# Attention with 64-row scores and normalised probabilities, norms by logarithm, and alternating output panels

## What is computed

```python
def first_block(x, ...):
    u = rmsnorm(h, norm_mix_g[layer])
    p = jnp.einsum('bsd,de->bse', u, w_in[layer]) + b_in[layer]
    aq, ak, av, hq, hf, hi, hg, gate_a, gate_b = split_columns(p)
    y_attn = sliding_window_sink_attention(aq, ak, av, attn_sinks[layer])
    y_hgrn = hgrn2_branch(hq, hf, hi, hg, lb_all[layer], hgrn_norm_g[layer])
    ya = jnp.einsum('bse,ed->bsd', y_attn, w_branch_attn[layer])
    yb = jnp.einsum('bse,ed->bsd', y_hgrn, w_branch_hgrn[layer])
    merged = jax.nn.sigmoid(gate_a) * ya + jax.nn.sigmoid(gate_b) * yb
    h = h + jnp.einsum('bsd,de->bse', merged, w_out[layer])
...
    # attention: a softmax over the keys and one sink
    probs = jax.nn.softmax(jnp.concatenate([scores, sink], axis=-1), axis=-1)[..., :-1]
    out = jnp.einsum('bhgqk,bnkhd->bnqhgd', probs.astype(v.dtype), vw)
...
    # end of the HGRN2 branch; the SSD mixer ends in a norm of the same form
    o = o * lax.rsqrt(jnp.mean(o * o, axis=-1, keepdims=True) + EPS)
    o = o.reshape(B, S, HGRN_WIDTH) * norm_g.astype(jnp.float32)
    o = o * jax.nn.sigmoid(hg.astype(jnp.float32))
```

## Time and profile before

| | us |
|---|---|
| median of 3 runs | 902.66 |
| lowest and highest | 901.04 and 906.4 |
| the profiled execution | 902.78 |
| its span on the core | 900.9 |
| TensorE busy | 838.6 |
| VectorE busy | 597.4 |
| ScalarE busy | 480.6 |

### The profile page before, as it was taken

How to read it: one execution, slowest core, us unless ns; L and a number is a source line. 1 busy time by engine, 2 the same in 40 slices (tenths; PEclk the granted TensorE clock), 3 DMA queues, 4 the chain that set the end, 5 groups by cost and what they waited for, 6 DMA issues and landing times. The chain is left out here.

```text
span 900.9 us, 14307 instructions
## 1 busy us (share of the span) xinstructions
PE 838.6 (93%) x5976; PEld 784.8 (87%) x5976; DVE 597.4 (66%) x754; ACT 480.6 (53%) x709; POOL 25.8 (3%) x43
## 2 busy tenths in 40 slices
PE   7999999969896989999999989998969899999996
PEld 6999989969895979999998879887947899999885
DVE  5554666477748748777779987674444588887653
ACT  6747768446633436344433456724443477666542
POOL 3400001000100000000000000000000000000000
PEclk9999999988998999999999998989979999999999
DMA  9644544426531555888778965533410386655621
GB/s 316 235 162 143 165 135 145 165 96 231 159 124 47 188 187 194 282 273 280 257 261 287 343 254 188 177 104 101 133 48 1 111 269 203 189 165 187 209 96 47
DMA packets 105952, 161.15 MB, mean 179 GB/s; under 512 B 4496, under 2 KB 51872, under 8 KB 105888
## 3 DMA queue, kind: packets, MB, share of 16 engines
q1 hardware_dynamic: 105888, 160.24, 53.6%
HBM read 159.16 MB, written 1.06 MB: 178 GB/s over the span
## 5 line engine op out<-in xcount | busy, mean ns | idle before, releaser
L1469 PE MATMUL ps<-p1H,wH 128*128 128x256 f32 x1256 | 366.0, 291 | 21.1 <-DVE wL L965 9.0
L965 DVE TENSOR_TENSOR wL<-raw,wH 128x2048 fp32r<-128x2048 f32 (+2 forms) x129 | 281.8, 2187 | 154.8 <-ACT wH L652 153.8
L1469 PE MATMUL ps<-p1L,wH 128*128 128x256 f32 x1256 | 360.8, 287 | 0.0
L1469 PE MATMUL ps<-p1H,wL 128*128 128x256 f32 x1256 | 360.6, 287 | 0.0
L652 ACT ACTIVATE wH<-raw 128x2048 fp32r<-128x2048 f32 (+1 forms) x124 | 231.3, 1869 | 152.5 <-PE ps L1469 75.1
L1469 PEld LDWEIGHTS ps<-p1H,wH 128*128 128x128 f32 x1256 | 246.5, 196 | 24.7 <-DVE wL L965 9.4
L1469 PEld LDWEIGHTS ps<-p1L,wH 128*128 128x128 f32 x1256 | 246.6, 196 | 0.4 <-issue 0.2
L1469 PEld LDWEIGHTS ps<-p1H,wL 128*128 128x128 f32 x1256 | 246.2, 196 | 0.0
L1472 PE MATMUL ps<-wH,zH 128*128 128x512 f32 x176 | 68.7, 390 | 0.0
L1472 PE MATMUL ps<-wL,zH 128*128 128x512 f32 x176 | 68.5, 389 | 0.0
L1472 PE MATMUL ps<-wH,zL 128*128 128x512 f32 x176 | 68.5, 389 | 0.0
(11 more groups left out here) (257 smaller groups left out, 1011.0 us busy)
## 6 DMA issues: line engine op xcount, KB each, us to landing
raw<-in_w_in SPq DMA_DIRECT2D x38, 1024.0 KB, 5.2
raw<-in_w_ada SPq DMA_DIRECT2D x24, 1024.0 KB, 5.3
raw<-in_w_up SPq DMA_DIRECT2D x44, 512.0 KB, 4.9
raw<-in_w_ffn_gate SPq DMA_DIRECT2D x22, 512.0 KB, 4.4
raw<-in_w_ffn_up SPq DMA_DIRECT2D x22, 512.0 KB, 5.5
raw<-in_w_ffn_down SPq DMA_DIRECT2D x10, 1024.0 KB, 5.6
raw<-in_w_down SPq DMA_DIRECT2D x10, 1024.0 KB, 5.1
raw<-in_w_out SPq DMA_DIRECT2D x8, 1024.0 KB, 5.1
```

What stands on the lines that cost most here:

```text
L965: return v.tensor_tensor(o, a, b, op)
L1469: last = mm(ps[:, t[1], 0:T], wt[:, slot, k, t[2]:t[2] + P], at_[:, k0 + k, :], start=st, stop=en)
```

## The change

*Attention.* The keys are no longer padded: the product of a head contracts over its 64 rows. The two heads of a pair lie in different halves of the rows and of the PSUM banks (`slot`), and the masks of both are written first. For keys that lie in the wrong half a swapped copy `aKS` is made. The value product has the values stationary, 64 columns for each head of a pair, and comes out transposed, so the item "yT" and its instructions are gone and "pv" does the split. The probabilities are normalised on VectorE in place, in the item "pt", ahead of TensorE's transposes, which now wait for `on.pn`. *Norms of the mixers.* HGRN2 and SSD take Ln and Exp(-0.5 x) on ScalarE for square root and reciprocal; the HGRN2 gain comes first (hD) and the product with the norm in an item of its own (hE); the split is done in halves. *Panels.* bh0 and bh1, and oo0 and oo1, alternate panel by panel, bh1 in PSUM banks 4 to 7. *Places.* Scores 7 stand ahead of pv 6; scores 8 are split in two (`scores_mm` for TensorE, ahead of the SSD sums); dt comes half a group earlier; a norm's gate sums and spreads come earlier with one copy for 256 columns instead of two for 128; the squares of norm 3 stand ahead of the evacuation of oo1; a low part of the first weights moves from GpSimd to VectorE; the ada item of f0 is gone and one stands behind part 4 of down1; the sums of ada move from f2, f4, f6, f8 to f3, f5, f7, f9. The line numbers after are higher by 3 to 14 (L965 becomes L971, L1415 becomes L1418, L1469 becomes L1480).

```diff
 def X(u):
     return [("pv", u - 1)] * (u > 0) + [("scores", u)] * (u < NU1)
 def Y(u):
-    return [("pt", u)] * (u < NU1) + [("yT", u - 1)] * (u > 0)
+    return [("pt", u)]
...
-    gemm("hq1", [("hD", 0)])
+    gemm("hq1", [("hD", 0)], [("hE", 0)])
...
-    gemm("ba1", [("hC", 1)], [("hsplit", 0), ("hD", 1), ("hsplit", 1)])
-    gemm("bh0")
-    gemm("bh1", [("merge", 0)], [("merge", 1)])
+    gemm("ba1", [("hC", 1)], [("hsplit", 0), ("hD", 1)])
+    gemm("bh0", [("hE", 1), ("hsplit", 1)], only=0)
+    gemm("bh1", only=0)
+    gemm("bh0", [], [("merge", 0)], only=1)
+    gemm("bh1", [], [("merge", 1)], only=1)
...
-    gemm("v2", [("pt", 6)], [("pv", 6), ("scores", 7)])
-    gemm("z", [("pt", 7), ("yT", 6)], [("pv", 7), ("yz",), ("scores", 8), ("ysum",), ("snorm",)])
-    gemm("oo0", [("pt", 8), ("yT", 7), ("pv", 8), ("yT", 8)])
-    gemm("oo1", [("squares", 3)], [("gate", 1), ("norm", 3)])
+    gemm("v2", [("pt", 6)], [("scores", 7), ("pv", 6)])
+    gemm("z", [("pt", 7)], [("pv", 7), ("yz",), ("scores_mm", 8), ("ysum",), ("snorm",), ("scores", 8)])
+    gemm("oo0", [("pt", 8)], only=0)
+    gemm("oo1", [("pv", 8)], only=0)
+    gemm("oo0", only=1)
+    gemm("oo1", [], [("norm", 3)], only=1)
...
-WITH_ADA += [(f"f{_i}", 0) for _i in range(NF)]
-WITH_ADA += [("down0", _i) for _i in range(1, 6)] + [("down1", _i) for _i in range(4)]
+WITH_ADA += [(f"f{_i}", 0) for _i in range(1, NF)]
+WITH_ADA += [("down0", _i) for _i in range(1, 6)] + [("down1", _i) for _i in range(5)]
...
-                elif k == "pv":
+                elif k == "pt":
                     u = e[1]
                     dve.wait_ge(on.probs, u + 1)
...
                     step(v.reciprocal(RD[:, u % 2, 0:nh], SU[:, u % 2, 0:nh]))
-                    dve.wait_ge(on.pv_psum, u + 1)
-                    if u:
-                        dve.wait_ge(on.yT_psum, u)
-                    tt(YT[:, 0:nh * DH].rearrange("p (h d) -> p h d", h=nh),
-                           ps[:, 6, 0:nh * DH].rearrange("p (h d) -> p h d", h=nh),
-                           RD[:, u % 2, 0:nh].unsqueeze(2).broadcast_to([P, nh, DH]), ALU.mult).then_inc(on.pv_done, 1)
+                    p = PR.rearrange("p (h b) n -> p h (b n)", h=nh)
+                    tt(p, p, RD[:, u % 2, 0:nh].unsqueeze(2).broadcast_to([P, nh, nk * P]), ALU.mult).then_inc(on.pn, 1)
...
                 elif k == "hD":
                     s = e[1]
+                    dve.wait_ge(on.o_sq, 2 * s + 2)
+                    for h in range(4):
+                        stt(T1[:, h], T1[:, h], pc("hgrn_norm_g", 4 * s + h), hG[:, h],
+                            ALU.mult, ALU.mult).then_inc(on.o_gain, 1)
+                elif k == "hE":
+                    s = e[1]
+                    dve.wait_ge(on.o_gain, 4 * s + 4)
                     for i in range(2):
-                        dve.wait_ge(on.o_rt, 2 * s + i + 1)
-                        step(v.reciprocal(T2[:, 2 * i:2 * i + 2], T2[:, 2 * i:2 * i + 2]))
-                        step(tt(T1[:, 2 * i:2 * i + 2], T1[:, 2 * i:2 * i + 2], T2[:, 2 * i:2 * i + 2], ALU.mult))
...
+                        dve.wait_ge(on.o_r, 2 * s + i + 1)
+                        tt(YF[s][:, 2 * i:2 * i + 2], T1[:, 2 * i:2 * i + 2], T2[:, 2 * i:2 * i + 2],
+                           ALU.mult).then_inc(on.hfin, 1)
...
-                    for hh in range(nh):
-                        h = h0 + hh
-                        o = sc45[:, hh * nk * P:(hh + 1) * nk * P]
...
-                            mm(o, identb[:], mask1[:, (2 - nk) * P:2 * P], start=True, stop=False)
-                            last = mm(o, aQ[:, h // 2, n * P:(n + 1) * P], aKZ[:, 2 * (h // 8) + h % 2, ks],
-                                      start=False, stop=True)
...
+                    for a in range(0, nh, 2):
+                        for hh in (a, a + 1):
+                            o = sc45[:, slot(nh, hh) * nk * P:(slot(nh, hh) + 1) * nk * P]
...
+                                mm(o, identb[:], mask1[:, (2 - nk) * P:2 * P], start=True, stop=False)
...
+                        for hh in (a, a + 1):
+                            h = h0 + hh
+                            r = slice(C * (h % 2), C * (h % 2) + C)
...
+                                kk = aK if h // 8 == h % 2 else aKS
+                                last = mm(o, aQ[r, h // 2, n * P:(n + 1) * P], kk[r, ks], start=False, stop=True)
...
                 elif k == "pt":
                     u = e[1]
-                    pe.wait_ge(on.probs, u + 1)
+                    pe.wait_ge(on.pn, u + 1)
...
-                            last = mm(ps[:, 6, hh * DH:(hh + 1) * DH], PT[:, hh * nk + kb, :], vv, start=kb == 0,
-                                      stop=kb == nk - 1)
+                                last = mm(ps[C * x:C * x + C, 6, pair * P:(pair + 1) * P], vv, PT[:, slot(nh, hh) * nk + kb, :],
+                                          start=kb == 0, stop=kb == nk - 1)
...
-                elif k == "yT":
-                    u = e[1]
-                    pe.wait_ge(on.pv_done, u + 1)
...
-                    for b in range(nh // 2):
-                        last = tr(ps[:, 4, b * P:(b + 1) * P], YT[:, b * P:(b + 1) * P])
-                    last.then_inc(on.yT_psum, 1)
```

More of the change, by code:

```diff
@@ L108, in timeline, with gemm @@
     ada = iter(range(24))
+    before_evac = {"oo1": [("squares", 3)]}
     later = []
-    def gemm(name, *after):
+    def gemm(name, *after, only=None):
         parts = len(GROUPS[name]["parts"])
-        for i in range(parts):
+        for i in range(parts) if only is None else (only,):
             tl.append(("panel", name, i))
@@ L1519, in _ @@
                 k = e[0]
-                if k == "gate":
-                    g = e[1]
-                    pe.wait_ge(on.w_lo, SIDX["ada", (3, 23)[g]] + 1)
-                    if g:
-                        pe.wait_ge(*EV["oo0", 1])
-                    for i in range(2):
-                        last = mm(ps[:, 2 * g + i, :], ones[:], ACC[10 * g + i], start=True, stop=True)
-                    last.then_inc(on.gate_psum, 1)
-                elif k == "panel":
+                if k == "panel":
                     panel(e[1], e[2])
```

223 lines of the change are left out of this document (113 added, 110 removed).

## The result

| | before | after |
|---|---|---|
| median, us | 902.5 (4 runs) | 915.84 (4 runs) |
| lowest and highest | 901.04, 906.4 | 914.57, 917.85 |
| profiled execution | 902.78 | 916.34 |
| mean granted clock | 0.967 | 0.960 |

A forecast was written before the change was run, and what follows sets the result against it. TensorE's work plus its waits was taken to bound the kernel. Stalls +46.4, their clock +18, TensorE's work -19.2, array changes +6.0, HGRN norm -20.7, moves -18.5 gave +12.0 on 902.8: 915 us, range 901 to 925.

The forecast's parts named there:

- the nine stalls: Attention: TensorE's transposes wait for VectorE's multiply, queued behind low half and ada, in nine units: +46.4 us.
- TensorE's work with the changes of array: Transposes gone, cheaper value products and overlapping scores: -19.2 us; changes between full and half array: +6.0 us.
- the clock: Lower clock behind each new stall, 9 x 2.0 = +18 us; clock regained where other gaps shrink or go.
- the gap at hq1: First HGRN half: without reciprocals the evacuation starts 5.7 us earlier, a gap of 2.0 stays; clock -2.6 us.
- The gap of 7.48: Second HGRN half, wait for operand halves at 289: falls away, -7.5 us and -1.5 of clock.
- the dt gap of 3.5: Second mixer, ahead of L1714: VectorE's dt chain comes half a group earlier, -2.7 us and clock -1.6.
- the SSD norm's 7.26: Wait at 663.12: without its reciprocal and with half the output panels ahead it becomes 3.9, -3.35 us.
- the ada item ahead of down1's evacuation: VectorE's ada multiplies, 3.11 us, ahead of down1's evacuation make norm 2 late: +2.8 us, lower bound 0.
- B: Rival: pairs of 64 rows don't overlap, so the scores win nothing, +8.7: 924 us; chance .12.
- C: Rival: the clock doesn't fall behind the new stalls, -18: 897 us, faster than before; chance .10.
- D: Rival: shorter waits on VectorE, array changes free, norm 2 not late: 906, down to 902 us; chance .15.
- E: Rival: further new waits, from late ScalarE copies and bh panels waiting for both HGRN split halves: 928 us; chance .08.

The follow-up runs named there:

- the early normalisation: Changed kernel with VectorE's sum, reciprocal and multiply of the probabilities moved right behind its maximum of the scores: 864.04 us, 0.957 of before.
- panels, with oo: Changed kernel with the panels of bh0, bh1 and of oo0, oo1 back in the old order, both panels of a group in a row: 925.29 us.
- functions, both mixers: Changed kernel with square root and reciprocal back in place of Ln and Exp in the HGRN and SSD norms: 926.87 us.
- the filler: Changed kernel with matmuls of overwritten result keeping TensorE at work in the nine stalls, ahead of the wait: 902.57 us.

## Why the prediction was right, and where it was right by luck

Set against the profiled executions, gap by gap, pitch by pitch:

| term, us | predicted | measured |
|---|---|---|
| the nine stalls | +46.4 | +40.7 |
| all other gaps of TensorE | -28.9 | 14.5 - 40.7 = -26.2 |
| TensorE's work with the changes of array | -13.2 | about -9.2 |
| the clock | +7.7 | about +5.8 |
| in no term | 0 | the rest: +2.6 |
| sum | +12.0 | +13.7 |

- **The mechanism** (normalisation behind low half and ada on VectorE, TensorE held at the transposes): right, shown by the early normalisation. **Its size** was 5.7 too large. The stalls are 6.0, 4.6, 6.7, 3.6, 6.2, 4.5, 4.4, 2.5 and 2.2 where 8.0, 4.9, 7.1, 3.9, 6.6, 4.9, 4.8, 2.9 and 3.3 were worked out. The first is off most: the scores end earlier, which lets VectorE start its low half at 56.03 instead of 57.88, while the panel above runs slower at the lower clock, so TensorE arrives later. The prediction had kept both in place.
- **The clock**: the term behind the stalls, 9 x 2.0 = 18, measured 13.3, and at the last stall the stretch behind has a clock of 1.00. The gains of clock elsewhere were taken at 10.3. One of them turned round: the dip behind the first scores was to go (-1.6), and the 10 us there have 62 matmuls and a clock of 0.66, where it was 0.83 before. The net can be read from the traces: TensorE's work at the lower clock went from 40.1 to 52.2 us. Of such a stretch 0.44 to 0.5 is lost (a matmul of the panels with 256 columns goes from 0.122 to 0.219 us on the mean), which gives 5.4 to 6.1 us for the +7.7 of the prediction. Its count of gaps was also misread: six waits of the kernel before are 2.3 us or longer, not eight, and behind the first of them, 3.57 at the start, the clock is 1.00. The low clock also stands behind waits of 1.53, 2.12 and 2.19, and not behind those of 1.79, 1.81 and 1.71.
- **TensorE's work**: here the term itself failed by 4 us. The value products won 9 x 0.70 = 6.3 with their changes of array, just the 7.9 - 1.6 that were forecast, and the 24 transposes their 2.6 (twelve in a row took 1.23, eight take 0.79). The scores won about 0.3, where 8.7 - 4.3 = 4.4 were forecast. (By the prediction's own figures the 8.7 should be 3 x 1.34 + 6 x 0.87 = 9.2.) A change was priced at 0.09 from a row with column halves (L1729). For the value products, which have column halves too, that is right: 1.03 us less eight times their pitch of 0.11 leaves 0.16 for two changes. The scores have row halves, and there the single records show three delays of 0.1 us in each pair: ahead of the first products, between the first and the second two (72.86 and 73.07, where the pitch is 0.11), and ahead of the next mask. That makes 0.30 for two changes, 0.15 each, and 48 x 0.06 = 3 us more than the prediction had. Also, a unit took 2.58 and 1.99 us before, not the 2.67 and 2.17 of the prediction. A unit of eight heads now takes 2.56, one of four 1.91. In the second mixer the one with one key block even became slower, 1.23 us a pair for 1.11.
- **In no term**: 2.6 us are placed nowhere. A part is likely the last matmul ahead of each new stall, which runs out its 0.28 us where the next would have followed after 0.12; nine times that is 1.4, an estimate.
- **The luck**: the stalls were taken 5.7 and the clock 1.9 too dear, the gains at the other gaps 2.7 and in TensorE's work 4.0 too large, and 2.6 had no term. These errors cancel down to 1.7 us, and that is how 915 came so near. The sign isn't luck: the stalls with their clock cost 40.7 + 13.3 = 54.0, and all gains together (26.2, 9.2 and 7.5 of clock) are 43.
- **The HGRN norm**: the gap at hq1 went from 7.78 to 2.12, -5.7 as worked out. The clock behind it gave less: 46 matmuls in 7 us, not 61. The gap of 7.48 went, for two reasons that the prediction named together and the runs priced at 9.5 (panels, with oo) and 11.0 us (functions, both mixers) against the changed kernel.
- **What moved**: the dt gap of 3.5 went; the SSD norm's 7.26 is 4.10 for 3.9 forecast; the ada item ahead of down1's evacuation costs 1.6 at norm 2 for 2.8 forecast. A likely reason, not tested, is that TensorE's sums at L1460 (2.79 us) cover a part.
- **The rivals**: B falls (the halves overlap), and what was lost at the scores is the price of the changes instead. The sign that was named for B, scores of a unit at 2.2 us and more, came all the same (2.56), so it could not tell the two apart; the pitch without changes between could. C falls: the clock over 7 us is 0.64 to 0.80 behind eight of the nine stalls, and the filler gives the price. D holds in part: the waits were shorter, and norm 2 is late by 1.3 us (2.97 + 0.94 for 0.46 + 2.12) and not by 2.8, but the changes of array were dearer, not free. E did not come.

## What to carry to other kernels

Where an engine walks one list, a stage that others wait for must stand where that engine would idle anyway: the same three instructions a unit cost 915.8 - 858.7 = 57 us behind a weight split and 5.4 ahead of it. Before adding a wait, look in the timeline for what stands ahead of its releaser and what that waits for. And a stall of TensorE of 2 to 7 us was here worth its length and 1.5 us more for the clock. A price read from one kind of row, such as that of a change to column halves, holds for that kind alone.

## What was not expected

- A change between full array and row halves costs 0.15 us, one between full array and column halves 0.08. The first ate nearly all that overlapping scores had won. One mask matmul for each bank took a unit of eight heads from 2.56 to 1.63 us.
- TensorE takes up a matmul for the other half of the rows past three that wait for theirs, so that up to four records of one half in a row cost nothing; eight cost 0.54 us a unit.
- Behind one and the same wait of 1.00 us the clock over 10 us was 0.66, 0.83 or 1.00 from kernel to kernel, and one kernel ran at 854.5 and 858.5 us with mean clocks of 0.988 and 0.981.
